# A four-plus-twelve-layer stack on one core: order of modulation pieces, recurrence, conv taps and vector sums

## The reference

```
c_act = silu(c)
for i in range(2):
    mod = (c_act @ ada_w[i] + ada_b[i])[:, None, :]
    sh_m, sc_m, gt_m, sh_f, sc_f, gt_f = jnp.split(mod, 6, axis=-1)
    h = rmsnorm(x, norm_g[i, 0]) * (1.0 + sc_m) + sh_m
    y = rglru_mixer(h, ...) if i == 0 else gla_mixer(h, ...)
    x = x + gt_m * rmsnorm(y, norm_g[i, 1])
    h = rmsnorm(x, norm_g[i, 2]) * (1.0 + sc_f) + sh_f
    y = conv_ffn(h, ffn_w_up[i], ffn_conv_w[i], ffn_conv_b[i], ffn_w_down[i])
    x = x + gt_f * rmsnorm(y, norm_g[i, 3])

def conv_ffn(h, w_up, conv_w, conv_b, w_down):
    u = causal_dwconv(h @ w_up, conv_w, conv_b)       # width 3 along the tokens
    g, val = jnp.split(u, 2, axis=-1)
    return (jax.nn.gelu(g) * val) @ w_down            # 2816 hidden channels

def rglru_mixer(...):
    gate_br, x_br = jnp.split(h @ w_in, 2, axis=-1)
    x_br = causal_dwconv(x_br, conv_w, conv_b)        # width 4
    r, i_g = sigmoid(x_br @ wa + ba), sigmoid(x_br @ wx + bx)     # in 4 blocks
    a = exp(-8 r softplus(-lam)); u = sqrt(1 - a*a) * (i_g * x_br)
    hs = scan(a * h_prev + u)                         # along the tokens
    return (gelu(gate_br) * hs) @ w_out
```

## Time and profile before

| | us |
|---|---|
| median of three runs | 2789.43 |
| the profiled execution | 2787.8 |
| its span | 2786.0 |
| TensorE busy | 2671.2 (96%) |
| GpSimd busy | 1971.7 (71%) |
| ScalarE busy | 1384.6 (50%) |
| VectorE busy | 1019.3 (37%) |

### The profile page before, as it was taken

How to read it: one execution, slowest core, us unless ns; L and a number is a source line. 1 busy time by engine, 2 the same in 40 slices (tenths; PEclk the granted TensorE clock), 3 DMA queues, 4 the chain that set the end, 5 groups by cost and what they waited for, 6 DMA issues and landing times.

```text
span 2786.0 us, 36003 instructions
## 1 busy us (share of the span) xinstructions
PE 2671.2 (96%) x15016; PEld 2281.1 (82%) x15016; DVE 1019.3 (37%) x1695; ACT 1384.6 (50%) x1667; POOL 1971.7 (71%) x432
## 2 busy tenths in 40 slices
PE   7889988799999999999999999999999999999998
PEld 4768887589888778888889888888878888877887
DVE  6867758343321364112123311211441121145312
ACT  3654454354544465445446454544544454455543
POOL 3567765287688765887877488787638878764785
PEclk8999989899999999999999999999999999999999
DMA  8678843265465533555545255555425555543453
GB/s 323 255 271 299 311 156 133 78 214 196 156 219 189 193 140 136 197 195 192 187 166 197 106 213 196 187 192 195 152 85 217 190 189 196 192 171 121 181 192 111
DMA packets 80391, 521.79 MB, mean 187 GB/s; under 512 B 8908, under 2 KB 9292, under 8 KB 24420
## 3 DMA queue, kind: packets, MB, share of 16 engines
q1 hardware_dynamic: 80228, 519.47, 51.7%
HBM read 518.38 MB, written 1.05 MB: 186 GB/s over the span
## 4 chain that ended last, share of the span: by engine, by line
PE 81%; DVE 9%; ACT 5%; DMA 2%; issue 1%; POOL 1%; SPq 0%; DVEq 0%; ACTq 0%
PE acc L565 16%; PE acc L526 15%; PE mb L503 10%; PE cb L503 10%; PE cb L478 8%; PE mb L505 5%; PE cb L505 5%; ACT whi L1142 2%; PE mb L618 2%; DVE AR L1836 2%; PE acc L830 1%; DMA raw<-in_w 1%; DMA AR<-in_a 1%; DVE hT L1786 1%; PE acc L478 1%
## 5 line engine op out<-in xcount | busy, mean ns | idle before, releaser
L2411 POOL TENSOR_TENSOR wlo<-raw,whi 128x2048 fp32r<-128x2048 f32 x428 | 1971.5, 4616 | 790.8 <-ACT whi L1142 710.9
L1142 ACT ACTIVATE whi<-raw 128x2048 fp32r<-128x2048 f32 x428 | 818.3, 1914 | 636.9 <-PE cb L503 245.6
L526 PE MATMUL acc<-whi,ARR 128*128 128x512 f32 x1312 | 367.4, 392 | 11.0 <-DVE ARR L1786 11.0
L503 PE MATMUL cb<-hT,whi 128*128 128x512 f32 x1280 | 335.3, 393 | 0.0
L503 PE MATMUL mb<-hT,whi 128*128 128x512 f32 x1280 | 334.1, 393 | 0.6 <-DVE ARR L1786 0.3
L526 PEld LDWEIGHTS acc<-whi,ARR 128*128 128x128 f32 x1312 | 246.3, 189 | 64.5 <-issue 11.0
L478 PE MATMUL cb<-hT,whi 128*128 128x256 f32 x1536 | 285.3, 288 | 14.0 <-DVE cb L1851 14.0
L565 PE MATMUL acc<-whi,hT 128*128 128x512 f32 (+2 forms) x928 | 260.4, 389 | 7.0 <-DVE hT L1786 5.7
L503 PEld LDWEIGHTS mb<-hT,whi 128*128 128x128 f32 x1280 | 230.2, 189 | 44.4 <-issue 3.6
L503 PEld LDWEIGHTS cb<-hT,whi 128*128 128x128 f32 x1280 | 229.6, 189 | 40.4
L478 PEld LDWEIGHTS cb<-hT,whi 128*128 128x128 f32 x1536 | 243.4, 195 | 22.4 <-issue 21.7
(11 more groups left out here) (320 smaller groups left out, 3407.7 us busy)
## 6 DMA issues: line engine op xcount, KB each, us to landing
raw<-in_w SPq DMA_DIRECT2D x436, 1024.0 KB, 4.8
AR<-in_a SPq DMA_DIRECT2D x80, 512.0 KB, 5.6
gb<-in_lng SPq DMA_DIRECT2D x12, 512.0 KB, 5.7
gb<-in_lnb SPq DMA_DIRECT2D x12, 512.0 KB, 6.6
gb<-in_normg SPq DMA_DIRECT2D x8, 512.0 KB, 7.1
x<-in_x SPq DMA_DIRECT2D x1, 1024.0 KB, 8.4
out<-x SPq DMA_DIRECT2D x2, 512.0 KB, 2.7
cn<-in_cn SPq DMA_DIRECT2D x1, 560.0 KB, 6.8
```

The costliest lines, as they stand in the source:

```text
L503: ins = pe.matmul(to[j], wh[:, w], hT[:, k, :], start=k == 0, stop=k == 7)
L526: ins = pe.matmul(acc[:, 2 * t + c, 0:c1 - c0], xs[y], a[:, kk * width + c0:kk * width + c1], start=first and kk == 0 and m == 0, stop=las ...
L1142: ac.activation(whi[i % NH][:, :], raw[u % NR][:, :], ACT.Copy).then_inc(*up(s_hi, ("hi", i)))
L2411: po.tensor_tensor(wlo[i % NH][:, :], raw[(i + NADA) % NR][:, :], whi[i % NH][:, :].bitcast(F32), ALU.subtract).then_inc(*up(s_lo, ("lo", i)))
```

## The change

Four things are moved; no instruction is added or taken away, apart from the waits between them.

1. `background()`: vector sums of RG-LRU's stage come after units 2, 5, 6, 7, 11 (before 2, 6, 8, 9, 11). Loads of pieces 5 to 20 are issued up to one unit sooner, those of 21 to 26 at units 16 and 17. Pieces 24 to 71 are worked on in units 20 to 42 (before 14 to 42). GLA's six sums of vectors 8 to 10 come three by three after its fourth and third unit from the end (before two by two after the last four's first three), on other banks.
2. `rglru`: VectorE does four pieces ahead of the convolution (before three), four instead of five after row 2, none between the recurrence's halves (before two), two at the end. ScalarE rounds units 12 and 13 both ahead of the recurrence's third quarter (before one ahead of the third and one ahead of the fourth).
3. `gated`: the Square, sqrt and gate product are cut off from `norm`. At the boundaries to conv0 and conv1 (b odd) the second tile's `gated` comes ahead of the first tile's copies (`turned`), and ScalarE's `highs` behind these; at the even ones the order stays.
4. `ffn`: in a conv FFN's head ScalarE does column 0's two taps together, then rounds a unit, then gelu, then column 1's first tap, then `high`; VectorE's low part of column 0 comes behind column 1's first taps.

```diff
@@ -149,10 +149,12 @@
     pieces = {}
-    sums = {2: [(2, 0)], 6: [(2, 1)], 8: [(3, 0)], 9: [(3, 1)], 11: [(4, 0)]}
+    sums = {2: [(2, 0)], 5: [(2, 1)], 6: [(3, 0)], 7: [(3, 1)], 11: [(4, 0)]}
     loads = {}
-    for n, h in zip(range(NB, 24), (4, 4, 5, 6, 7, 8, 9, 9, 9, 10, 10, 10, 11, 11, 11, 12, 12, 12, 13, 13, 14)):
+    for n, h in zip(range(NB, 27), (4, 4, 4, 5, 6, 7, 8, 9, 9, 9, 10, 10, 10, 10, 10, 11, 11, 11, 16, 16, 16, 17, 17, 17)):
         loads.setdefault(h, []).append(n)
-    after = [FIRST[1] + (i * 29) // 48 for i in range(48)] + [FIRST[3] + 3 + 3 * i for i in range(8)]
+
+    after = [FIRST[1] + 6 + (i * 23) // 48 for i in range(48)] + [FIRST[3] + 3 + 3 * i for i in range(8)]
     for n, h in enumerate(after, 24):
         pieces.setdefault(h, []).append(n)
-        loads.setdefault(18 if n < 27 else FIRST[3] + 4 if 72 <= n < 75 else after[n - 27] + 6, []).append(n)
+        if n >= 27:
+            loads.setdefault(FIRST[3] + 4 if 72 <= n < 75 else after[n - 27] + 6, []).append(n)
         v, half = 2 + n // 8, n // 4 % 2
@@ -160,4 +162,3 @@
             sums.setdefault(h + 2, []).append((v, half))
-    for i, v in enumerate((8, 9, 10)):
-        sums[FIRST[3] - 4 + i] = [(v, 0), (v, 1)]
+    sums[FIRST[3] - 4], sums[FIRST[3] - 3] = [(8, 0), (8, 1), (9, 0)], [(9, 1), (10, 0), (10, 1)]
     return pieces, sums, loads, 24 + len(after)
@@ -457,3 +458,3 @@
 
-                to = claim(bank("cb" if v < 2 or v in (8, 9, 10) and half else "mb"), ("vec", v, half))
+                to = claim(bank("cb" if v < 2 or (v, half) in ((8, 1), (9, 0), (10, 0), (10, 1)) else "mb"), ("vec", v, half))
                 q.wait_ge(*on("added", v, half))
@@ -1151,12 +1152,15 @@
 
+            def gated(b, t):
+
+                ss, s = small(f"ss{t}", 1), small(f"rs{t}", 1)
+                q.wait_ge(*on("full", (("sum", b - 1), t)))
+                ac.activation(z[:, t, :], acc_t(t), ACT.Square, accum_out=ss).then_inc(*up(s_ac, ("gsq", b, t)))
+                q.wait_ge(*now(s_ac))
+                ac.activation(s, ss, ACT.Sqrt, bias=ep6, scale=1.0 / D).then_inc(*up(s_ac, ("groot", b, t)))
+
             def norm(b, t):
 
-                gate, _, scale = mods[b]
+                _, _, scale = mods[b]
                 ss, s = small(f"ss{t}", 1), small(f"rs{t}", 1)
                 q.wait_ge(*on("eps"))
-                if gate is not None:
-                    q.wait_ge(*on("full", (("sum", b - 1), t)))
-                    ac.activation(z[:, t, :], acc_t(t), ACT.Square, accum_out=ss).then_inc(*up(s_ac, ("gsq", b, t)))
-                    q.wait_ge(*now(s_ac))
-                    ac.activation(s, ss, ACT.Sqrt, bias=ep6, scale=1.0 / D).then_inc(*up(s_ac, ("groot", b, t)))
                 if scale is not None:
@@ -1188,8 +1192,22 @@
                 h = FIRST[b]
-                for t in range(2):
-                    (norm if b < 5 else layer_norm)(b, t)
-                    if t == 0 and b:
+                if b < 5:
+                    gated(b, 0)
+                    norm(b, 0)
+                    if b % 2:
+                        gated(b, 1)
+                        turned(b, 0)
+                        highs(h - 2 + NH)
+                    else:
+
                         highs(h - 2 + NH)
-                    if t == 0 and b < LAST:
                         turned(b, 0)
+                        gated(b, 1)
+                    norm(b, 1)
+                else:
+                    for t in range(2):
+                        layer_norm(b, t)
+                        if t == 0:
+                            highs(h - 2 + NH)
+                            if b < LAST:
+                                turned(b, 0)
 
@@ -1233,7 +1251,6 @@
 
-                def gate(p, key, between=None):
+                def gate(p, key):
                     if conv:
-                        taps(p, 0, key, tmp(0, p % 2))
-                        if between:
-                            between()
+                        if p > 1:
+                            taps(p, 0, key, tmp(0, p % 2))
                         q.wait_ge(*on("conv", n, p, 0))
@@ -1262,4 +1279,7 @@
                         unit(h - 2)
-                        gate(0, ("turn0", n, 0), lambda: unit(h - 1))
+                        taps(0, 0, ("turn0", n, 0), tmp(0, 0))
                         taps(0, 1, ("turn0", n, 1), tmp(2, 0))
+                        unit(h - 1)
+                        gate(0, ("turn0", n, 0))
+                        taps(1, 0, ("up", n, 1, 0), tmp(0, 1))
                         high(0, ("turn0", n, 1))
@@ -1350,4 +1370,5 @@
                 for j in range(4):
-                    if j > 1:
-                        unit(h + 6 + j)
+                    if j == 2:
+                        unit(h + 8)
+                        unit(h + 9)
                     q.wait_ge(*on("rgy", j))
@@ -1711,2 +1732,11 @@
 
+            def gated(b, t):
+
+                gate = mods[b][0]
+                yt = acc_t(t)
+                q.wait_ge(*on("gsq", b, t))
+                q.wait_ge(*on("mod", gate))
+                dv.tensor_tensor(yt, yt, mod_row(gate), ALU.mult).then_inc(
+                    *up(s_dv, ("gated", b, t), *([("rowfree", row_of[gate])] if t else [])))
+
             def norm(b, t):
@@ -1719,7 +1749,5 @@
                 if gate is not None:
-                    q.wait_ge(*on("gsq", b, t))
-                    q.wait_ge(*on("mod", gate))
-                    dv.tensor_tensor(yt, yt, mod_row(gate), ALU.mult).then_inc(*up(s_dv, *freed(gate)))
                     q.wait_ge(*on("groot", b, t))
                     dv.reciprocal(s, s).then_inc(*up(s_dv))
+                    q.wait_ge(*on("gated", b, t))
                     chain()
@@ -1806,4 +1834,15 @@
                     return
+                if b < 5:
+                    gated(b, 0)
+                    norm(b, 0)
+                    if b % 2 == 0:
+
+                        turned(b, 0)
+                    gated(b, 1)
+                    if b % 2:
+                        turned(b, 0)
+                    norm(b, 1)
+                    return
                 for t in range(2):
-                    (norm if b < 5 else layer_norm)(b, t)
+                    layer_norm(b, t)
                     if t == 0 and b < LAST:
@@ -1872,3 +1911,2 @@
                         product(0, ("turn0", n, 0), ("turn0", n, 1))
-                        low(0, ("turn0", n, 1))
                         unit(h)
@@ -1882,2 +1920,4 @@
                         taps(p, 0, ("up", n, p, 0), tmp(0, p % 2))
+                        if p == 1:
+                            low(0, ("turn0", n, 1))
                     else:
@@ -1936,3 +1976,3 @@
 
-                some(3)
+                some(4)
                 for j in range(4):
@@ -1972,3 +2012,3 @@
                 vector_half(2, 1)
-                some(5)
+                some(4)
                 vector_half(3, 0)
@@ -1999,3 +2039,2 @@
                     if hf == 0:
-                        some(2)
                         vector_half(3, 1)
@@ -2003,2 +2042,3 @@
                 vector_half(4, 0)
+                some(2)
 
```

## The result

The kernel after takes 2777.71 us at the median of five runs (2774.98 to 2782.52), the kernel before 2791.15. The two medians lie 13.4 us apart; the ratio of the runs, by which I go, is 0.9962 with a 95% interval of 0.9951 to 0.9972: faster by 0.38%, some 10.6 us (7.8 to 13.7). The forecast was 2776, range 2762 to 2789, by a sum of 13.6 us.

A forecast was written before the change was run, and what follows sets the result against it. TensorE, busy 96% of the span, was taken as the bound, so only its idle time and half-clock stretches could be won. 3.4 + 11.4 - 13.5 + 7.9 + 4.4 = 13.6; 2787.8 - 13.6 + 1.6 gives 2776 us, range 2762 to 2789.

The forecast's parts named there:

- RG-LRU and boundary: RG-LRU stage up to conv0's first block end: earlier sums, moved pieces and earlier Square and gate product gain 3.4 us.
- The meeting with GpSimd: RG-LRU's recurrence: products meet back-to-back GpSimd subtractions; second product ends at 118.4, output units start at 120.1 against 121.98.
- Conv0's head: No pieces up to unit 19 and the new tap order shorten it from 40.97 to 29.5 us: gain 11.4.
- Conv0's columns: Conv0's body: 48 pieces in 22 units instead of 28, 6 per column not 5; loss 13.5 us, bounds 3 to 22.
- the clock: Conv0's body: gaps of 3 to 4 us bring the lower clock two times, costing 2 us.
- the replay: Conv0's body: replaying a column's VectorE order with six pieces puts the seven columns at 138.9 us, against 128.35.
- the flat 5.1 us for a load: Conv0's body: each piece load assumed to take 5.1 us behind the use of the buffer.
- GLA's end: All six vector sums ahead of the close; transposes 5.8 us sooner, block end 550.0 against 557.85: gain 7.9.
- conv1's head: Idle 2.98 us goes, and the half-clock stretch of 1.5 behind it: gain 4.4, bounds 2 to 5.
- R1: Conv0's body nearly free, the sixth piece falling into VectorE's idle time: loss 4 instead of 13.5, 2766 us; chance 0.20.
- R2: VectorE becomes the bound of conv0's body: 27 us loss makes the total even, 33 gives 2795; chance 0.12.
- R3: Port lock and late loads: RG-LRU loses 2, conv0's head gains only 7; 2786, no change; chance 0.18.

The follow-up runs named there:

- experiment 6: Kernel after, with two waits added so GpSimd's subtractions for units 11 and 13 start behind VectorE's recurrence products: 2774.33 us.
- experiment 11: Kernel after with the edits of experiment 8 (fourth buffer) and experiment 9 (spread pieces), GpSimd's two waits, and ScalarE's first copies ahead of its last gelu: 2757.53 us.
- experiment 3: Kernel after, with the second tile's Square and gate product back behind the first tile's transposed copies: 2779.84 us.
- experiment 1: Kernel after, with conv0's 48 background pieces back in units 14 to 42 as before: 2771.95 us.
- experiment 4: Kernel after, with the old order of taps in conv0's and conv1's heads: 2786.16 us.
- experiments 2 to 6: Five variants of the kernel after; the one not named singly has RG-LRU's part undone and the new boundary kept: 2780.79 us.
- half loads: Kernel after, with loads of pieces 27 to 71 bringing only the first half of each piece, VectorE's instructions unchanged: 2772.78 us.
- experiment 2: Kernel after, with GLA's six last vector sums back at one vector a unit in its last units: 2783.76 us.
- experiment 12: Kernel of experiment 11, with GpSimd held for the second half's products one subtraction sooner, at unit 12 instead of 13: 2760.65 us.
- experiment 9: Kernel after, with the 48 pieces placed by VectorE's idle time: five in units 17 to 19, 43 over units 20 to 44: 2766.56 us.
- experiment 8: Kernel after, with a fourth buffer for conv0's piece loads, six pieces a column kept: 2779.56 us.

## Why the prediction was right, and where it was off

**RG-LRU and boundary, 3.4 forecast, 3.2 measured.** Step by step, with the 1.7 us of later start taken off: outputs at 119.1 (forecast 120.1), the sum behind piece 19 at 135.0 (136.9), first transposes 149.8 (151.3), second 159.0 (159.1), block end 166.7 (166.5). The meeting with GpSimd came where it was put. In the first half it cost 1 us less than forecast: one of the two products came through between the subtractions, where the forecast had both behind them. The forecast "without any such meeting" was 147.2 for the transposes; experiment 6 has them at 147.18, in part by luck: its output units start at 117.86, and experiment 11, with output units from 114.66, has the transposes at 147.31 all the same. The fit of 3.2 to 3.4 is closer than one profile can tell, with 115.6 to 119.0 us for the same program. What ended the wait for the second transposes was not the chain, though: TensorE's own matmuls at half clock did, and the gain of the earlier Square is hidden there (experiment 3). The Trainium skill, "SBUF — State Buffer", section "SBUF: two separate sides", has the exclusive port pair, held for a whole instruction by whichever starts first. Experiment 6 agrees (0.70 us for 4.86).

**Conv0's head, 11.4 and 11.2.** The two causes are now apart: the pieces 7.6 (experiment 1), the order of taps 2.7 (experiment 4), and 0.9 that comes only with both.

**Conv0's columns: the term that was mis-sized.** Forecast 138.9 and 2 for the clock, in all 12.5 over before; measured 17.2 in this trace. Five more profiles with the pieces in the same places gave 142.1 to 145.9 (experiments 2 to 6); the mean of the six is 144.0, a loss of 15.7. Two terms were too small. The first is the clock: TensorE worked 3.1 to 15.4 us of these columns at half clock in the six profiles, 7.0 on average, which is about 3.5 us where I had put 2. The second is the replay: without the clock's part the six give 138.2 to 142.1, 140.5 on average, for 138.9. In this trace it is 142.1. By columns the replay said 82.2 for the first four and 56.7 for the last three; after has 83.4 and 62.1, half loads 84.5 and 57.6. In the last three the flat 5.1 us for a load failed: five loads took 8.1 to 8.9, and VectorE waited 2.91 and 2.36 us for two of them. That is not so in every run: experiment 2, with whole loads, has 57.9 there. The replay also went by 6 pieces a column in 22 units; it is 23 units (20 to 42) and 6.3 a column, nine pieces more than before in the seven columns and not seven.

The mechanism was right, but in less pure a form than one number says. As estimates, against a before of 126.2 without the clock's part, the loss of 15.7 is some 10 us for the pieces' place in VectorE's order (what half loads leave), 4 to 5 for late loads, and 1.4 for the clock (3.5 for the 2.1 of before). The Trainium skill, "DMA: Bandwidth & Descriptors", section "Anatomy of one DMA", would have 3.2 us for a full load and 2.6 for half a one, as estimates for another issue path. The medians are 5.6 and 3.3, so the row was the better guide. Where a load is waited for, the spread counts and not the median.

**GLA's end, 7.9 and 7.0; conv1's head, 4.4 and 4.2.** Both as argued: sums about 5 and the gate product 1.5; the 2.98 us gone, the half-clock stretch with it. The transposes came at 541.92 with 1.61 left to wait, inside the forecast 2. The prediction's own terms, 5.8, 1.1 and 1.6, add up to 8.5 and not to 7.9; measured are 4.8 up to the transposes and 2.2 behind them.

**Rivals.** R1 (loss 4) and R2 (over 27) are both out: 15.7. R3 named the right place, the lock, but the stage gained in spite of it. The sum of 13.6 lies at the upper end of what the ratio allows, 7.8 to 13.7 us; with the columns at their mean size it would have been 10.4, against 10.6. That 2776 lies so near to 2777.71 is in part luck: it starts from 2789.4, which is 1.1 us above what 2777.71 and the ratio give for before (2788.3), and so covers a third of the 3 us by which the gain falls short.

**Left open.** Why the same order of pieces gives 142.1 in one profile and 145.9 in another. Part is the clock: the 145.9 has 15.4 us of work at half clock, the 142.1 has 3.1. Why the loads and these stretches fall elsewhere each time stays open. The split of the loss into order, loads and clock rests on single profiles. Whether experiment 12's loss would go if piece 21's load were queued ahead of that weights' load was not tried.

## What to carry to other kernels

Background work on an engine costs little where that engine is idle anyway, and nearly its whole length when it is queued ahead of work that another engine waits for: look up the idle stretches in the trace and place it piece by piece, as experiment 9 did, instead of clearing one stage and packing the next. A moved step lands among new neighbours, so look at what the other engine on the same port does at the new time. And before holding an engine back, name the buffers that it would have freed, and the queue whose head waits for them. The same holds for a new buffer: its first load can block a queue for longer than the buffer saves (experiment 8).

## What the runs showed of the hardware

- A VectorE product with two SBUF operands, alone 0.70 us, started at 114.32, 0.7 us behind a GpSimd subtraction (113.62 to 118.62), and ended at 119.18: it stood until the subtraction was over. Between two back-to-back subtractions VectorE was let in: the product that had waited since 113.07 ended at 114.21, and the second subtraction took 5.00 us, where the median is 4.62. The second pair shows the same (0.81 us, then 5.06 for the subtraction and 4.99 for the product).
- Three loads of 512 KB, issued at 203.7 to 205.2 right behind three of 1 MB (202.4 to 203.3), landed 10.3 to 11.4 us after issue (experiment 8); the one ahead of them, at 201.94, took 3.1. In after's columns the median is 5.6.
- Idle gaps of the same size have different ends: in after's columns 3.4 us at 1.2 GHz followed the gaps of 4.14, 3.20 and 1.88 us, and none those of 2.56 and 2.06.
